# Windowed attention on one core: packed score matmuls, one-pass score extraction, a new order of copies

## The reference, cut to what matters

```python
s_win = jnp.einsum('bhqd,bhrkd->bhqrk', qr, kr).astype(jnp.float32) * ATTN_SCALE
s_win = s_win + bias.transpose(0, 2, 1, 3).astype(jnp.float32)[None]
s_win = jnp.where(col_ok[:, None, :], s_win, NEG_INF).reshape(b, h, GRID_W, kh * GRID_W)
s_ctx = jnp.einsum('bhqd,bhld->bhql', qr, k_ctx).astype(jnp.float32) * ATTN_SCALE
p = jax.nn.softmax(jnp.concatenate([s_win, s_ctx], axis=-1), axis=-1).astype(v.dtype)
o = jnp.einsum('bhqn,bhnd->bhqd', p[..., :kh * GRID_W], vr.reshape(b, h, kh * GRID_W, d))
return o + jnp.einsum('bhql,bhld->bhqd', p[..., kh * GRID_W:], v_ctx)
```

## Time and profile before

| | us |
|---|---|
| median of three runs | 2514.53 (2510.34 to 2516.4) |
| the profiled execution | 2510.91 |
| its span | 2509.1 |
| TensorE busy | 2382.1 (95%) |
| VectorE busy | 1296.3 (52%) |
| ScalarE busy | 725.6 (29%) |
| GpSimd busy | 657.8 (26%) |

### The profile page before, as it was taken

The page is one execution under the profiler, slowest core; times in us unless marked ns, Lnnn a source line. Parts: engine busy times, 40 slices in busy tenths (PEclk is TensorE's granted clock), DMA queues, the critical chain, the costliest instruction groups (busy, mean ns, idle before and its releaser), DMA issues.

```text
span 2509.1 us, 50765 instructions
## 1 busy us (share of the span) xinstructions
PE 2382.1 (95%) x21658; PEld 1964.0 (78%) x21658; DVE 1296.3 (52%) x2077; ACT 725.6 (29%) x1189; POOL 657.8 (26%) x283
## 2 busy tenths in 40 slices
PE   5899999999999998889999998999999999999997
PEld 4777878788888887888745687888888888888886
DVE  4575657527568667895543323634333433443344
ACT  5273644634455553333300001201100110011002
POOL 2022020111211111222000244434344444444341
PEclk9999999999999999999989998999999999999999
DMA  6313111022266786676423310111111111111112
GB/s 281 109 35 106 55 60 62 28 95 76 93 193 193 202 230 191 196 204 183 154 75 115 119 35 26 34 34 43 35 42 34 43 34 43 34 42 37 40 34 93
DMA packets 224561, 234.53 MB, mean 93 GB/s; under 512 B 143922, under 2 KB 178866, under 8 KB 222898
## 3 DMA queue, kind: packets, MB, share of 16 engines
q1 hardware_dynamic: 199090, 229.55, 28.4%
q10 hardware_dynamic: 25344, 3.15, 0.8%
HBM read 173.80 MB, written 57.02 MB: 92 GB/s over the span
## 4 chain that ended last, share of the span: by engine, by line
PE 81%; DVE 8%; issue 3%; ACT 2%; DMA 2%; SPq 1%; ACTq 1%; POOL 1%; DVEq 0%; POOLq 0%
PE PS L878 20%; PE PS L879 20%; PE PS L880 20%; PE PS L1354 6%; PE PS L1022 3%; PE PS L994 2%; DVE buffer L2081 2%; PE PS L1008 1%; DVE buffer L2080 1%; PE PS L996 1%; DMA buffer<-in_w_ada_first 1%; ACTq L1729 1%; PE PS L1074 1%; PE PS L1164 1%; PE PS L1326 1%
## 5 line engine op out<-in xcount | busy, mean ns | idle before, releaser
L878 PE MATMUL PS<-buffer,buffer 128*128 128x512 f32 (+1 forms) x2784 | 997.5, 358 | 10.2 <-DVE buffer L1976 3.4
L879 PE MATMUL PS<-buffer,buffer 128*128 128x512 f32 (+1 forms) x2784 | 987.8, 355 | 1.7 <-issue 1.7
L880 PE MATMUL PS<-buffer,buffer 128*128 128x512 f32 (+1 forms) x2784 | 987.8, 355 | 0.0
L878 PEld LDWEIGHTS PS<-buffer,buffer 128*128 128x128 f32 x2784 | 525.6, 189 | 97.3 <-issue 17.0
L880 PEld LDWEIGHTS PS<-buffer,buffer 128*128 128x128 f32 x2784 | 525.6, 189 | 78.8 <-issue 2.1
L879 PEld LDWEIGHTS PS<-buffer,buffer 128*128 128x128 f32 x2784 | 525.9, 189 | 75.2 <-issue 1.0
L2366 POOL TENSOR_TENSOR buffer<-buffer,buffer 128x1024 fp32r<-128x1024 f32 x76 | 184.0, 2421 | 816.8 <-PE PS L880 510.4
L2309 DVE SCALAR_TENSOR_TENSOR buffer<-PS,buffer,buffer 128x512 f32<-128x512 f32 (+1 forms) x264 | 158.5, 655 | 151.4 <-PE PS L880 151.4
L2367 POOL TENSOR_TENSOR buffer<-buffer,buffer 128x1024 fp32r<-128x1024 f32 x76 | 194.1, 2554 | 6.0
L2285 DVE TENSOR_SCALAR buffer<-buffer,buffer 128x1281 f32<-128x1281 f32 x22 | 34.8, 1582 | 286.6 <-ACT buffer L1810 286.6
L1810 ACT ACTIVATE buffer<-PS 128x512 f32<-128x512 f32 (+1 forms) x66 | 30.0, 529 | 504.3 <-PE PS L880 504.3
(11 more groups left out here) (228 smaller groups left out, 2796.9 us busy)
## 6 DMA issues: line engine op xcount, KB each, us to landing
buffer<-in_w_up SPq DMA_DIRECT2D x44, 512.0 KB, 3.3
buffer<-in_w_in SPq DMA_DIRECT2D x42, 512.0 KB, 5.2
ops_kept<-buffer SPq DMA_DIRECT2D x40, 512.0 KB, 4.6
buffer<-ops_kept SPq DMA_DIRECT2D x80, 256.0 KB, 3.4
buffer<-in_w_ada SPq DMA_DIRECT2D x32, 512.0 KB, 6.3
buffer<-rkv_kept SPq DMA_DIRECT2D x120, 128.0 KB, 3.3
buffer<-in_w_down SPq DMA_DIRECT2D x22, 512.0 KB, 3.3
buffer<-in_x SPq DMA_DIRECT2D x20, 512.0 KB, 7.6
```

The source lines that it names most:

```text
L878: mm(out, w_hi, x_hi, start=start, stop=False)
L879: mm(out, w_hi, x_lo, start=False, stop=False)
L880: return mm(out, w_lo, x_hi, start=False, stop=stop)
```

## The change

- `qbd` becomes `qT`: the queries as they come, 64 features of head 0 on partitions 0 to 63, those of head 1 on 64 to 127. The scores of two units u and u+1 are made together (`scores(u)`, for even u, two turns ahead), with 64 by 64 weights: the even unit uses the quarters of the array on the diagonal, the odd unit those off it, so the odd unit's heads lie swapped on the output partitions. `bias_swapped` is a copy of the bias with the heads swapped, made by two DMAs per pair.
- The score matmuls move to banks 0 to 5 (`win_bank`, `ctx_scores`); the window transposes go to bank 6, the 2 context transposes and the results share bank 7.
- VectorE takes scores out of PSUM (`scores_out`): one instruction each for window and context computes -(score + bias)/8 and keeps a running minimum, each followed by an instruction that reads the accumulated value. ScalarE's copy of the context scores and VectorE's maximum are gone. The exponential has scale -1.
- The values are made by column halves (`values(u)`): per block of 128 keys two matmuls with 128 by 64 weights and 64 columns, one for each head. VectorE copies the result of both heads in one instruction.
- ScalarE copies the 2 context blocks of the transposed probabilities (256 columns), VectorE the 4 window blocks (512 columns). Before it was the other way round (512 on ScalarE, 256 on VectorE).
- Order in a turn: ScalarE copies first, then scales, then takes the exponential. VectorE: reciprocal, result copy, transposed copy, scores of the next unit. TensorE: scores (even turns), values of t-3, transposes of t-2; the last 2 transposes wait for the copied result of unit t-3.
- GpSimd no longer clears `qbd`.

The core of the diff:

```diff
-    put("win_ok", ok)
+    put("win_ok", ok / SCALE)
...
+        zeros = const("zero").to_broadcast([P, CTX])
...
-        qbd = s2(NU, P)
+        qT = s2(T)
...
+        bias_swapped = s2(NDR, 64)
...
+        O_AT = 2 * P
+
+        def win_bank(u):
+
+            return 3 * (u // 2 % 2) + 2 * (u % 2)
+
+        def ctx_scores(u):
+
+            s = u // 2 % 2
+            if u < 4:
+                return PS[:, 3 * s + 1 + u % 2, 0:CTX]
+            return PS[:, 3 * s + 1, u % 2 * CTX:(u % 2 + 1) * CTX]
...
+                sp.wait_ge(proj_out_d, i * PROJ_D + 5)
+                for hh in range(2):
+                    sp.dma_start(one_head(bias_swapped, hh), one_head(bias, 1 - hh)).then_inc(vodd_in, 16)
...
+                def hold(sem, base, count):
+
+                    pe.reg_add(awaited, base, count)
+                    pe.wait_ge(consts_in, 32)
+                    pe.wait_ge(sem, awaited)
+
+                def scores(u):
+
+                    if u >= 4:
+                        hold(ctx_out, units, u - 2)
+
+                    def one(v, part):
+                        for h in range(2):
+                            f, o = slice(64 * h, 64 * h + 64), slice(64 * (h ^ v % 2), 64 * (h ^ v % 2) + 64)
+                            if part == 0:
+                                r0, _ = unit_window(v)
+                                ins = mm(PS[o, win_bank(v), :], qT[f, v * 64:v * 64 + 64], kT[f, CTX + GRID * r0:CTX + GRID * r0 + 512],
+                                         start=True, stop=True)
+                            else:
+                                keys = kcT if v >= 4 else kT[:, 0:CTX]
+                                ins = mm(ctx_scores(v)[o], qT[f, v * 64:v * 64 + 64], keys[f], start=True, stop=True)
+                        return ins
+
+                    if u >= 4:
+                        one(u, 0)
+                    ins = one(u + 1, 1)
+                    if u >= 4:
+                        ins.then_inc(side_scored, 1)
+                        one(u + 1, 0)
+                        hold(side_scored, pairs, (u - 2) // 2)
+                    one(u, 1).then_inc(scored, 1)
...
+                def values(u):
+
+                    nb = 2 if u < 4 else 6
+                    pe.wait_ge(pt_out_a, i * NU + u + 1)
+                    if u >= 4:
+                        pe.wait_ge(pt_out_d, i * ROWS + (u - 3))
+                    if u == 4:
+                        pe.wait_ge(vodd_in, i * 64 + 64)
+                    for b, (src, at) in enumerate(unit_keys(u)):
+                        for h in range(2):
+                            q = 64 * (h ^ u % 2)
+                            ins = mm(PS[64 * h:64 * h + 64, 7, O_AT:O_AT + 64], src[:, at, 64 * h:64 * h + 64],
+                                     pT[u % 2][:, b, q:q + 64], start=(b == 0), stop=(b == nb - 1))
+                    ins.then_inc(o_done, 1)
+
+                def transposes(u):
+
+                    pe.wait_ge(p_ready, i * NU + u + 1)
+                    for b in range(0 if u < 4 else 4):
+                        pe.transpose(PS[:, 6, b * P:(b + 1) * P], scr[:, u % 3, b * P:(b + 1) * P], ident)
+                    if u >= 1:
+                        pe.wait_ge(o_out, i * 2 * NU + 2 * u)
+                    for b in range(2):
+                        ins = pe.transpose(PS[:, 7, b * P:(b + 1) * P], scr[:, u % 3, 512 + b * P:512 + (b + 1) * P], ident)
+                    ins.then_inc(pt_done, 1)
...
+                scores(0)
                 for t in range(NU + 3):
-                    if t < NU:
...
+                    if t % 2 == 0 and t + 2 < NU:
+                        scores(t + 2)
+                    if t >= 3:
+                        values(t - 3)
                     if 2 <= t < NU + 2:
-                        u = t - 2
-                        nb = 2 if u < 4 else 6
...
-                            pe.wait_ge(vodd_in, i * 32 + 32)
-                        for b, (src, at) in enumerate(unit_keys(u)):
...
+                        transposes(t - 2)
...
-                    src = PS[:, g, 0:n].rearrange("p (u t) -> p u t", t=64)
-                    dst = qbd[:, t0 // 64:(t0 + n) // 64, :]
-                    A.step(act.activation(dst[0:64, :, 0:64], src[0:64], ACT.Copy))
-                    act.activation(dst[64:128, :, 64:128], src[64:128], ACT.Copy).then_inc(proj_out_a, 1)
+                    act.activation(qT[:, t0:t0 + n], PS[:, g, 0:n], ACT.Copy).then_inc(proj_out_a, 1)
...
+                for t in range(NU + 2):
+                    if t >= 2:
+                        u = t - 2
+                        at = 0 if u < 4 else 4
+                        act.wait_ge(pt_done, i * NU + u + 1)
+                        if u >= 2:
+                            act.wait_ge(o_done, i * NU + u)
+                        act.activation(pT[u % 2][:, at:at + 2, :].rearrange("p b n -> p (b n)"), PS[:, 7, 0:2 * P], ACT.Copy) \
+                            .then_inc(pt_out_a, 1)
                     if 1 <= t <= NU:
                         u = t - 1
                         lo = 512 if u < 4 else 0
                         act.wait_ge(recip_ready, i * NU + u + 1)
                         act.activation(scr[:, u % 3, lo:768], scr[:, u % 3, lo:768], ACT.Copy,
                                        scale=rowstat[:, u % 3, 2:3]).then_inc(p_ready, 1)
...
                     if t < NU:
                         u = t
                         lo = 512 if u < 4 else 0
-                        act.wait_ge(max_ready, i * NU + u + 1)
-                        act.activation(scr[:, u % 3, lo:768], scr[:, u % 3, lo:768], ACT.Exp,
+                        act.wait_ge(ctx_out, i * NU + u + 1)
+                        act.activation(scr[:, u % 3, lo:768], scr[:, u % 3, lo:768], ACT.Exp, scale=-1.0,
                                        bias=rowstat[:, u % 3, 0:1], accum_out=rowstat[:, u % 3, 1:2]).then_inc(exp_done, 1)
...
+                def scores_out(u):
+
+                    if u >= 3:
+                        dve.wait_ge(pt_done, i * NU + (u - 2))
+                    if u == 5:
+                        dve.wait_ge(vodd_in, i * 64 + 64)
+                    hold(scored, pairs, u // 2 + 1)
+                    least = 3.0e38
+                    if u >= 4:
+                        _, b0 = unit_window(u)
+                        least = rowstat[:, u % 3, 3:4]
+                        dve.tensor_tensor_reduce(scr[:, u % 3, 0:512], PS[:, win_bank(u), :],
+                                                 (bias, bias_swapped)[u % 2][:, b0 // 64:b0 // 64 + 8, :].rearrange("p d c -> p (d c)"),
+                                                 -SCALE, 3.0e38, ALU.add, ALU.min, least).then_inc(win_out, 1)
+                        hold(win_out, rows, u - 3)
+                    dve.tensor_tensor_reduce(scr[:, u % 3, 512:768], ctx_scores(u), zeros, -SCALE, least, ALU.add, ALU.min,
+                                             rowstat[:, u % 3, 0:1]).then_inc(ctx_out, 1)
+
...
                 for t in range(NU + 3):
                     if 1 <= t <= NU:
                         u = t - 1
                         dve.wait_ge(exp_done, i * NU + u + 1)
                         dve.reciprocal(rowstat[:, u % 3, 2:3], rowstat[:, u % 3, 1:2]).then_inc(recip_ready, 1)
-                    if t < NU:
-                        u, bank = t, 2 * (t % 2)
-                        lo = 512 if u < 4 else 0
-                        dve.wait_ge(ctx_out, i * NU + u + 1)
-                        if u >= 4:
-                            _, b0 = unit_window(u)
-                            stt(scr[:, u % 3, 0:512], PS[:, bank, :], SCALE,
-                                bias[:, b0 // 64:b0 // 64 + 8, :].rearrange("p d c -> p (d c)"), ALU.mult, ALU.add) \
-                                .then_inc(win_out, 1)
-                            dve.wait_ge(win_out, i * ROWS + u - 3)
-                        if u >= 3:
-                            dve.wait_ge(p_ready, i * NU + u - 2)
-                        dve.tensor_reduce(rowstat[:, u % 3, 0:1], scr[:, u % 3, lo:768], AX.X, ALU.max, negate=True) \
...
-                            dve.wait_ge(pt_done, i * NU + u + 1)
-                            dve.wait_ge(o_done, i * NU + u)
-                            dve.tensor_copy(pT[u % 2][:, 4:6, :].rearrange("p b n -> p (b n)"), PS[:, 5, 0:256]).then_inc(pt_out_d, 1)
                     if t >= 3:
                         u = t - 3
                         dve.wait_ge(o_done, i * NU + u + 2)
-                        for h in range(2):
-                            dst = ybT[:, bass.ds(i, 1), u * 64:(u + 1) * 64].rearrange("p a t -> p (a t)")
-                            dve.tensor_copy(dst[64 * h:64 * h + 64], PS[64 * h:64 * h + 64, 6, 64 * h:64 * h + 64]) \
-                                .then_inc(o_out, 1)
...
+                        dst = ybT[:, bass.ds(i, 1), u * 64:(u + 1) * 64].rearrange("p a t -> p (a t)")
```

(10 more changed lines are left out.)

89 lines of the change are left out of this document (26 added, 63 removed).

## The result

The changed kernel takes **2539.91 us** (median of 5 runs, 2529.4 to 2550.0) against 2514.53 us (5 runs); the ratio is 1.010, with a 95% interval of 1.007 to 1.014. The forecast was 2502 us, in a range up to 2520, and "slower" had a chance of 0.22. The profiled execution took 2539.91 us, with a span of 2538.1 where it was 2509.1.

What follows compares the result with a forecast made beforehand. TensorE bounded the old units at 3.29 us each; afterwards a 3.07 us chain of waits would. Saving 3.1 us a pair, 12.4 for four, gave 2498.5 for a profiled-like execution, 3.6 below the median: 2502 us, range 2492 to 2520.

Steps and rivals of the forecast that it cites:

- Later stages only start earlier: Stages behind the units: the change was taken to do nothing there but let them start earlier; nothing charged.
- the sum: Attention pair, start to last result copy: turns -2.3 us, tail -1.6, even turns +0.8, together -3.1, -12.4 for four.
- TensorE's score pair: Scores of two units on TensorE: 8 records with 512 and 8 with 256 columns, four at a time, 1.2 us.
- the rival that they would go two by two: Score matmuls not four at a time: 2.4 instead of 1.2 us a pair of units, 2535 us; chance 0.12.
- Even turns: Turns in which TensorE also makes scores: 0.07 us ahead of the chain, 0.1 charged on each.
- a difference of over 0.3 between even and odd turns: Sign that would show the forecast wrong: turn periods in the units differing by over 0.3 us.
- The charge of 0.1 on 8 even turns: Units of a pair: 0.1 us added on each of 8 even turns for TensorE's thin margin, +0.8 in all.
- Start of a pair: Context units up to the exponential of u = 4: + 9.1 us where it was 9.07, nothing won or lost.
- Tail: Behind a pair's last exponential to the last result copy: 6.3 to 6.4 us against 8.02, -1.6.
- The chain of 3.07 us: Latent turn: ScalarE copy, scaling, exponential, VectorE reciprocal and result copy, TensorE's last two transposes in sequence; period 3.07 us.
- The extraction pair: VectorE taking window and context scores out of PSUM: 0.80 and 0.53, together 1.33 us a turn.
- The clock: Rival: TensorE, less busy, drops to half clock, 4.3 us a unit, 2575 us (a tenth of the time, 2510); chance 0.08.

Runs made afterwards that it cites:

- e1: The changed kernel with TensorE's attention loop written out four times instead of looped, which also removes its register waits: 2506.5 us.
- e5: The kernel before with 160 small matmuls, no part of the computation, added ahead of every pair's units in TensorE's loop: 2716.4 us.
- e6: The kernel before with the same 160 added matmuls a pair as e5, TensorE's attention loop written out four times: 2673.1 us.
- e7: e1 with the odd unit's context scores issued first, ahead of the window scores of both units: 2501.2 us.
- e8: e1 with window scores of both units in the even turn and context scores of both in the odd turn: 2494.4 us.
- e3: The kernel before with TensorE's attention loop written out four times: 2514.65 us.
- the padded ones: The kernel before with small matmuls added per pair: 60 (2573.7 us), 110 (2658.8), 160 (e5, 2716.4), or 160 with the loop written out (e6, 2673.1).
- e2: The changed kernel with TensorE's attention loop run twice over two pairs of heads each, one way back instead of three: 2524.8 us.
- e4: e1 with the odd unit's window scores moved from the even turn to the odd turn behind it: 2501.3 us.

## Why the prediction was wrong, step by step

- **The step that failed by being absent.** "Later stages only start earlier", and the sum ends with the last result copy of a pair: between that and the next projection nothing was charged. With the loop written out, 33 us go (2539.9 to 2506.5, e1); the traces place some 27 of them there, in e1 as in e5 against e6. Per way back: the gap of 0.53 us became 4.3 in pair 1, the second gap is 0.6 to 2.0, and at half clock the projections lose 2 us in pair 1 (some two dozen 0.21 apart and not 0.12) and more in pair 2. What was needed to suspect it, a body that grows from 1,345 to 1,906 instructions, follows from the two programs; its price was in no row, and a rival "the longer body doesn't fit" would have been its place. Without this step the range would have held: e1 lies in it, 4.5 us above the forecast, but with 1.7 us gained in a pair where 3.1 was forecast (112.35 us between exponentials 0 of pairs 1 and 2 before, 110.65 in e1).
- **TensorE's score pair: 1.2 us forecast (1.25 up to the values), 1.85 measured to the start of the values.** Two errors in one term. The 16 records do lie four at a time, and both heads of a unit do write one bank, so the rival that they would go two by two (2535 us) is out by its mechanism, though it named nearly the time. But 0.1 a record with 512 columns, twice the 0.05 of rows 6, makes 0.4 for a round of four; measured, a round takes 0.48, and with the context scores 1.44 for a unit. And the wait on `side_scored` was costed at nothing: 0.30 us by e7, in the order in which the scores stood; the register instructions of the waits, 0.10 by e1, too.
- **Even turns**: 3.17 forecast, 3.57 measured. The text named a difference of over 0.3 between even and odd turns as the sign of being wrong, and it is 0.54. TensorE had 0.07 us to spare by the forecast, and the 0.6 of the score pair went into the five long even turns among a pair's latent ones nearly whole (3.57 - 3.03 = 0.54). Over the 15 latent turns of pair 3: 540.06 - 491.71 = 48.35 us, where 46.85 was forecast and 48.34 measured before. The gain of the units is used up there. The charge of 0.1 on 8 even turns has its counterpart in five turns by 0.54.
- **Start of a pair**: 9.1 forecast, 491.71 - 481.67 = 10.04. The second score pair stands in a short context turn, 0.6 us longer than laid out, and its values and the result copy behind it come later. In e8, where its context scores stand one turn later, exponential 0 to exponential 4 takes 7.50 us (8.74 after, 7.42 before).
- **Tail**: 6.35 forecast, 546.67 - 540.06 = 6.61, against 8.02 before. Right in kind, 0.25 us short: values to result copy take 1.06.
- **The chain of 3.07 us**: right, 0.04 above what was measured. Odd turns take 3.03, and in e8 all do. The extraction pair takes 1.33 us as forecast (503.98 to 505.31), the values 0.85 with the change of tiling (0.70 + 0.16), the ScalarE copy follows the transposes at once.
- **The clock**: given as a rival for the units as a whole; it is 1.00 in steady turns. It fell in other places, above. (Its 2575 is reckoned from 2498.5; from the forecast of 2502 it would be 2579.)
- **What e1 leaves.** The terms above are worth some 1.3 us a pair there, since its even turns (3.48) and pair starts are a little shorter than with the register waits, together 5 us. In its profiled execution the clock fell in three pairs (next section), for 1.3 us each at least, and pair 0 began 2.6 us later (first exponential 122.25, before 119.61; 122.44 in e3, which has nothing of the change). The rest of the program, the same code in all of these kernels but the padded ones, took from 1978.9 to 1991.4 us in their profiled executions (1981.8 in e1, 1988.6 before), so a single profile says nothing of 5 us there, and the terms can't be closed to better than that. That e2, with one of three ways back, lost 18 us to e1 is placed in part: 14.4 lie between exponentials 0 of pairs 0 and 3 (349.0 against 334.6), 9.6 of them across the way back, some 2 in its register waits and about 1 in more falls of the clock; for the rest there is no row.

## What to carry to other kernels

When an engine's loop gets longer, look at the length of its body as at a resource: here 1,585 instructions for TensorE go back at no cost and 1,785 don't, and each way back then costs about 9 us in the traces, the half clock behind the gap included. Splitting matmuls over quarters of the array multiplies instructions, so the two go together. On TensorE, a wait for an earlier piece of its own work behaved as if it also waited for what was issued ahead of that piece (1.75 us for the score group, 1.45 with the piece first): put the piece first, and spread matmuls over turns until no turn has more than the chain leaves it.

## What the hardware showed that I had not expected

- The limit is sharp: at 1,585 instructions no gap and no loss, at 1,785 three gaps of 4.7 us on average, and time lost behind them.
- After a gap of 4 to 5 us TensorE ran at 0.50 of its clock, the lower of its two levels (1.2 GHz), for 3.5 to 9.4 us. It came back while TensorE was busy in pairs 2 and 3 (317.0 and 433.0 us), and in pair 1 at about 194 us, where it stood in the second gap.
- The same fall, without a gap, comes near the start of the units, where the context units leave TensorE idle. In e7's pair 1 (windows of TensorE, columns as above):

```profile
238.00:240.00 2.00, 0.61 (x10) 1.00 0.98 383
240.00:241.00 1.00, 1.00 (x8) 0.53 0.59 242
...
243.00:244.00 1.00, 1.00 (x16) 0.77 0.00 0
```

 It was busy for 0.61 of the 2 us ahead, and then at half clock for over 3; the turn took 4.22 us and not 3.1. The four pairs of the changed kernel show it once, those of e1 three times, of e7 four, of e4 and e8 never. It also fell in e2 three times and in e3 twice (0.59 from 236 to 240 us, 0.67 from 461 to 464), which has nothing of the change, and not in the profiled execution of the kernel before. It costs 0.8 to 2.5 us each time (least and most in e2); what decides whether it comes at one of these starts wasn't tried.
- Work alone doesn't always bring the clock back: in e5 and e6 it stayed at 0.50 for some 70 us of the added matmuls in pair 0, with TensorE busy for 70.9 of 71.7 us, and was 1.00 for the same matmuls in later pairs (e6, 300.2 to 336.2 us, 0.112 a record). Why it differs is open.
